# Ten input tiles scaled by VectorE in one instruction and transposed by DMA, in place of ScalarE, TensorE and a PSUM eviction

## What is computed

```python
def _rmsnorm(x, g):
    y = xf * lax.rsqrt(jnp.mean(xf * xf, axis=-1, keepdims=True) + EPS)
    return (y * g).astype(x.dtype)

u = _rmsnorm(h, g_mix)                       # D_MODEL = 1024
proj = jnp.einsum('ntd,de->nte', u, w_in)    # 1024 x 9216
a_b, a_c, a_h, a_z, b_v, b_g, b_z, gate_a, gate_b = jnp.split(proj, SPLITS, axis=-1)
v = b_v * jax.nn.sigmoid(b_g)                # input of the 31-tap convolution
...
h = h + m @ w_o
h = h + sigmoid(rmsnorm(h, g_ple) @ w_pg) * (p @ w_pe)
```

## Time and profile before

| | |
|---|---|
| median of 3 runs | 884.12 us (883.93 to 884.82) |
| the profiled execution | 888.18 us |
| its slowest core (core 1), first to last instruction | 886.6 us |
| TensorE busy | 855.5 us, 96% |
| VectorE, ScalarE, GpSimd busy | 508.5, 301.1, 145.0 us |
| shortest span of a core (core 0) | 877.5 us |

### The profile page before, as it was taken

How to read it: one execution, slowest core, us unless ns; L and a number is a source line. 1 busy time by engine, 2 the same in 40 slices (tenths; PEclk the granted TensorE clock), 3 DMA queues, 4 the chain that set the end, 5 groups by cost and what they waited for, 6 DMA issues and landing times.

```text
span 886.6 us, 15264 instructions; the slowest of 8 cores (877.5 to 886.6 us)
## 1 busy us (share of the span) xinstructions
PE 855.5 (96%) x4970; PEld 443.1 (50%) x4970; DVE 508.5 (57%) x791; ACT 301.1 (34%) x565; POOL 145.0 (16%) x274
## 2 busy tenths in 40 slices
PE   7999988999999999999999999999999999999993
PEld 4886544555444545454554444444445444444441
DVE  2455334566997777777777733333333235777775
ACT  4773223355344332423323321111111112444442
POOL 3142101100101101010210101110001001344441
PEclk9999999999999999999999999999999999999997
DMA  9977999987302123030313155521222044867642
GB/s 196 260 145 100 163 154 193 148 134 110 81 0 48 24 37 60 13 61 1 60 17 57 18 161 95 96 39 33 48 48 42 13 96 101 207 172 181 175 126 95
DMA packets 93964, 84.42 MB, mean 95 GB/s; under 512 B 53280, under 2 KB 74784, under 8 KB 93344
## 3 DMA queue, kind: packets, MB, share of 16 engines
q1 hardware_dynamic: 66112, 52.29, 25.2%
q0 software_dynamic: 27776, 31.17, 23.8%
HBM read 86.80 MB, written 15.61 MB: 116 GB/s over the span
## 4 chain that ended last, share of the span: by engine, by line
PE 85%; DMA 5%; SPq 3%; issue 2%; ACT 2%; DVE 2%; POOL 1%; DVEq 0%; POOLq 0%; ACTq 0%
PE ps L409 67%; PE ps L849 7%; PE ps L870 6%; SPq L346 3%; PE ps L604 3%; PE ps L876 1%; DMA t_v<-vd 1%; DMA vd<-t_vrow 1%; DMA t_x<-x 1%; PE ps L672 1%; DMA t_ring<-w_ob 1%; ACT t_xb L484 0%; PE ps L498 0%; DMA t_cb<-t_c 0%; ACT t_xb L424 0%
## 5 line engine op out<-in xcount | busy, mean ns | idle before, releaser
L409 PE MATMUL ps<-t_uT,t_ring 128*128 128x512 bf16 (+2 forms) x3200 | 543.5, 330 | 0.9 <-DMA t_ring<-w_in 0.7
L409 PEld LDWEIGHTS ps<-t_uT,t_ring 128*128 128x128 bf16 x3200 | 279.6, 98 | 252.5 <-issue 3.0
L823 DVE TENSOR_TENSOR t_tmp<-ps,t_tmp 128x512 f32<-128x512 f32 (+1 forms) x80 | 48.7, 610 | 151.7 <-PE ps L409 151.1
L343 POOL DMA_DIRECT2D t_ring<-w_in x72 | 38.8, 540 | 392.4 <-PE ps L409 389.6
L820 ACT ACTIVATE t_tmp<-ps 128x512 f32<-128x512 f32 (+1 forms) x80 | 42.3, 532 | 177.6 <-PE ps L409 177.6
L781 ACT ACTIVATE t_tmp<-t_tmp,t_vid 128x512 f32<-128x512 f32 (+1 forms) x40 | 29.9, 749 | 125.0 <-DVE t_tmp L778 125.0
L535 DVE TENSOR_TENSOR t_vrow<-ps,t_tmp 128x512 bf16<-128x512 f32 (+2 forms) x52 | 25.2, 485 | 79.1 <-PE ps L409 34.1
L409 PE MATMUL ps<-t_cb,t_ring 128*128 128x512 bf16 (+1 forms) x320 | 65.4, 347 | 0.3 <-DMA t_ring<-w_ob 0.3
L409 PE MATMUL ps<-t_yaT,t_ring 128*128 128x512 bf16 (+1 forms) x320 | 65.4, 347 | 0.0
L849 PE MATMUL ps<-t_wo_t,t_cb 128*128 128x512 bf16 x272 | 61.5, 379 | 0.0
L870 PE MATMUL ps<-t_wpg_t,t_u2T 128*128 128x512 bf16 x256 | 57.9, 379 | 0.0
(11 more groups left out here) (99 smaller groups left out, 755.1 us busy)
## 6 DMA issues: line engine op xcount, KB each, us to landing
t_ring<-w_in POOLq DMA_DIRECT2D x72, 256.0 KB, 5.9
t_x<-x SPq DMA_DIRECT2D x17, 512.0 KB, 8.6
t_xs<-x SPq DMA_DIRECT2D x17, 512.0 KB, 5.7
t_cb<-t_c SPq DMA_DIRECT2D x64, 128.0 KB, 6.5
y<-t_yt SPq DMA_DIRECT2D x16, 512.0 KB, 3.7
vd<-t_vrow SPq DMA_DIRECT2D x28, 128.0 KB, 4.6
t_v<-vd SPq DMA_DIRECT2D x7, 512.0 KB, 10.1
t_ring<-w_oa POOLq DMA_DIRECT2D x8, 256.0 KB, 5.9
```

Source lines behind the costliest of these rows:

```text
L343: S.add("pool", lambda e: e.dma_start(out=out, in_=in_), reads=reads, writes=list(writes) + [swq()], dma=key)
L409: S.add("pe", lambda e, k=k: e.matmul(ps[:, b, 0:n], lhsT=ring[k_ring][:, k, :], rhs=rhs_fn(k), start=(k == 0), stop=(k == NCH - 1)), read ...
L823: S.add("dve", lambda e, p=p, t=t: e.tensor_tensor(out=tmp[t][:, 0:n], in0=ps[:, p, 0:n], in1=tmp[t][:, 0:n], op=ALU.mult), reads=[f"ps{p} ...
```

## The change

From preparation step i = 7 on (tiles 6 to 15, ten tiles) `s1_a2` has a new body and `s1_b` returns at once. VectorE multiplies the float32 tile by the column `rsd` and by the row `g_mix` in one instruction and writes bf16 into `xb1`; after the load six steps ahead, SyncE issues a DMA transpose of `xb1` into the tile's columns of `uT`. The row of `g_mix`, broadcast to 128 partitions on the host, is a new input of 512 KB; it is loaded once by SyncE right after `s1_a2(1)`, into memory that the accumulators `accs`/`accq` use later. The first seven steps stay as they were.

`s1_step` now calls `s1_a2(i)` and `s1_a1(i + 1)` for i from 9 on; steps 8's scaling and 9's squares have moved into `FIRST`. The eight steps are called one after the other at P0 j=0, P0 j=2, P1 j=0, 1, 2, P2 j=0, 2, and P3 j=0 (ten calls before, the last at P3 j=2).

```diff
+        gmix = at("gmix", [128, D], F32, o_acc)
...
+        FIRST_DT = 7
...
         def s1_a2(i):
...
+            if i >= FIRST_DT:
+                t = TILES[i]
+                si, o = t // 4, 128 * (t % 4)
+                S.add("dve", lambda e: e.scalar_tensor_tensor(
+                    out=xb1[bq][:], in0=xs1[xq][:], scalar=rs_ap, in1=gmix[:], op0=ALU.mult, op1=ALU.mult),
+                    reads=[f"x1{xq}", rs_res, "gmix"], writes=[f"xb1{bq}", f"xb1h{bq}"])
+                if xnext[0] < len(TILES):
+                    s1_load(xnext[0])
+                S.add("sp", lambda e: e.dma_start_transpose(out=uT[si][:, :, o:o + 128], in_=xb1[bq][:]),
+                      reads=[f"xb1{bq}", f"xb1h{bq}"], writes=[f"uT{t}", f"uTh{t}"], dma=f"uT{bq}")
+                return
...
+            if i == 1:
+                sdma(gmix[:], gmix_d, [], ["gmix"], "gmix")
 
         def s1_b(i):
+            if i >= FIRST_DT:
+                return
...
-        nxt = [7]
+        nxt = [9]
 
         def s1_step():
             i = nxt[0]
-            if i < len(TILES):
-                nxt[0] += 1
-                s1_b(i)
-                s1_a2(i + 1)
-                s1_a1(i + 2)
+            nxt[0] += 1
+            s1_a2(i)
+            s1_a1(i + 1)
...
-                 (s1_a2, 6), (2, 4), (3, 0), (s1_b, 6), (s1_a1, 7), (3, 1), (s1_a2, 7), (3, 2), (s1_a1, 8), (3, 3), (3, 4)]
+                 (s1_a2, 6), (2, 4), (3, 0), (s1_b, 6), (s1_a1, 7), (3, 1), (s1_a2, 7), (3, 2), (s1_a1, 8), (3, 3), (s1_a2, 8),
+                 (s1_a1, 9), (3, 4)]
...
-        PIECES += [(1, 0, 256, (1, 0, 1, 0)), (1, 256, 256, (1, 1, 1, 0)), (2, 0, 256, (1, 1, 0, 1)),
-                   (2, 256, 256, (1, 0, 1, 0)), (3, 0, 512, (0, 0, 0, 0))]
+        PIECES += [(1, 0, 256, (1, 0, 1, 0)), (1, 256, 256, (1, 1, 1, 0)), (2, 0, 256, (1, 0, 1, 0)),
+                   (2, 256, 256, (1, 0, 0, 0)), (3, 0, 512, (0, 0, 0, 0))]
```

More of the change, by code:

```diff
@@ L180, in build_program @@
     gple_d = din("gple", [128, D])
+    gmix_d = din("gmix", [128, D])
     gfin_d = din("gfin", [128, D])
@@ L1052, in build_program @@
                 sdma(hista[:], sa_d, [], ["hista"], "hista")
+        assert nxt[0] == len(TILES)
         S.alias([f"cq{q}_{g}" for q in range(4, 8) for g in range(NQ)] + [f"c{q}_4" for q in range(4, 8)], X1_RES)
+        S.alias([f"acc{c}{si}" for c in "sq" for si in range(5)], ["gmix"])
         jobs = [(j, si) for j in range(4, 8) for si in (4, 0, 1, 2, 3)]
@@ L1237 @@
     gple = np.ascontiguousarray(np.broadcast_to(f(g_ple[0])[None, :], (128, D)))
+    gmix = np.ascontiguousarray(np.broadcast_to(f(g_mix[0])[None, :], (128, D)))
     gfin = np.ascontiguousarray(np.broadcast_to(f(g_final)[None, :], (128, D)))
@@ L1248 @@
     shared = dict(w_in=cols(w_in[0]), w_oa=cols(w_out_a[0]), w_ob=cols(w_out_b[0]), w_o=rows(w_o[0]),
-                  w_pg=rows(w_pg[0]), w_pe=rows(w_pe[0]), tw=tw, mask=mask, vecs=vecs, gfin=gfin, gple=gple)
+                  w_pg=rows(w_pg[0]), w_pe=rows(w_pe[0]), tw=tw, mask=mask, vecs=vecs, gfin=gfin, gple=gple, gmix=gmix)
     def phases(a):
```

## The result

The changed kernel takes **891.36 us** (median of 5 runs, 890.08 to 908.53) against 884.82 for the kernel before beside it (also 5 runs). In the longest run two cores of one die had a mean granted clock of 0.96 where the others had 0.99, so the ratio is taken from the other four: 1.0068, 95% interval 1.0054 to 1.0082. That is 6.0 us slower where 4.9 less was forecast. What TensorE was to save it did save. The waits for transposes came larger than priced and in more places, and the row of `g_mix` cost more.

What follows compares the result with a forecast made beforehand. TensorE was taken to set the pace; -6.3 us for removed transposes, +0.2 for the row of `g_mix` and +1.2 for the wait before P4 gave -4.9, so 884.12 became 879.2 us, range 876.5 to 885.0.

Steps and rivals of the forecast that it cites:

- The rest ... 6.3 us is what ten tiles cost: TensorE, 42.50 us to the last removed transpose's end: 30.74 less 24.43 of projections saves 6.3 us, at least 4.5.
- VectorE 1.28 us, ScalarE relieved: Ten VectorE evictions of 1.214 us become instructions of 1.278, 0.6 us more but hidden; ScalarE loses 11.5 us, adding no gain.
- these instructions now stand in front of later products: On VectorE, a late new instruction holds back products and PSUM banks; TensorE runs four projections, 7 us, ahead before that costs.
- The row of `g_mix` ... 0.2 us: 512 KB load on the x queue delays the loads behind it 2.4 us; cost 0.2 us, bounds nothing and 2.4.
- A queue that has little else to do: SyncE's queue takes ten transposes of 1.22 us issue time, 12 us; a `vst` store goes out about 1.2 us later.
- The tiles before the last have at least one more projection of lead: P1's transposes go out before P0; for P2 and P3 five projections or more lie between issue and need.
- The wait before P4: TensorE waits for the last tile's transpose at the start of P4: 1.2 us, bounds 0.2 and 4.5.
- It fits, but barely: DMA time in the shortened stretch: 28.9 us plus 11.7 for ten transposes, 40.6 us in 32, a share of 1.27.
- rival 1: DMA engines overfull in the shortened stretch, TensorE waits at P2, P3 and P4; about 883.5 us, no change; chance 0.16.
- rival 2: Last tile's transpose caught behind other packets at P4's start, TensorE waits 11.2 us; 889.2 us, slower; chance 0.12.
- Two signs that the text names against itself: Forecast is wrong if TensorE waits for `uT` at P2 or P3 too, or transposes take 9 us or more.
- Everything after P4 moves forward as it is: After P4 start, later loads and stores are issued when TensorE, ScalarE and VectorE reach them, so all moves forward.

Runs made afterwards that it cites:

- nosws: Changed kernel with mask, `tw`, `vsd` stores, history and `vs` loads behind the last transpose, and transposes ahead of x loads on SyncE; 1.0113 to the kernel before.
- dt11: Changed kernel, only steps 11 to 16 by DMA, GpSimd's loads early, `g_mix` behind step 8, scratch for squares, steps packed into P0 to P2; 0.9968, 882.8 us.
- dt9: dt11 with eight tiles by DMA (steps 9 to 16) and `g_mix` behind step 6; 1.0034 to the kernel before.
- dt11n: dt11 with `mask`, `tw` and the history in their old place after P0; 1.0020 to the kernel before.
- nosw: Changed kernel with mask, `tw`, `vsd` stores and loads of history and `vs` behind the last transpose; 1.0133 to the kernel before.
- bearly: Kernel before, with only the early loads of `mask`, `tw` and history, behind the squares of step 5; 0.9993 to the kernel before.

## Why the prediction was wrong

- **"The rest ... 6.3 us is what ten tiles cost": right.** Eight of the ten tiles lay between P1 and P4. The kernel before takes 28.1 us from the one to the other and nosws 22.9: 5.2 us, 0.65 a tile for the 0.63 of the text. dt11, with six tiles, takes 23.9: 4.2 us, 0.70 a tile.
- **VectorE 1.28 us, ScalarE relieved: right.** 1.280 us measured, ScalarE 10.0 us less busy on core 1 (291.1 for 301.1; the text has 11.5). That VectorE's new work is hidden held in its sum but not in its order: "these instructions now stand in front of later products" looked at what stands behind them. What stands before them is a product that a store of `vst` can hold. It did so for 2.03 us before P4 on core 1, hidden there behind SyncE's queue, and it is on the chain of dt9.
- **"The row of `g_mix` ... 0.2 us": mis-sized.** It measured 1.9 us with an interval of 0.3 to 3.6, near the upper bound of 2.4 in the text. With the row alone P1 to P4 already come 1.2 to 1.4 us later, so the stretch did not take up the delay; the range had it, the sum did not.
- **"A queue that has little else to do": wrong.** The ten transposes held SyncE for 22 to 29 us in sum, by core, where the text had 12. The median was 2.3 to 2.4 us on cores 0 and 1, the longest 10.9, and stores, loads and the next transpose stood behind it. On core 1 this put the last transpose's issue 1.65 us behind its tile.
- **"The tiles before the last have at least one more projection of lead": the step that failed most.** P1 was 2.9 us later than before (1.1 of it already at P0), and TensorE waited 1.5 to 2.8 us in front of it on every core; in front of P2 it waited on seven of eight, 0.6 to 2.2 us and 9.23 on core 0. The lead itself was there: step 8's transpose was issued 3.7 to 4.9 us before P1 was due. But P1 began only 5.6 to 7.5 us after that issue. The lead had been set against a landing of 2.9 us, from the last stage of one core, where one transpose was in flight at a time; on the other cores some take up to 5.3 even there. The median landing in this stretch was 5.2 to 6.0 us.
- **The wait before P4, taken as 1.2 us in bounds of 0.2 to 4.5.** Seven cores waited 2.5 to 3.9 us, inside the bounds but near their upper end. For the median core the P3 to P4 distance grew from 8.7 to 12.0 us.
- **"It fits, but barely": the size was right, the conclusion wrong.** The share was worked out at 1.27 and measured at 1.21 on core 1 (1.11 on core 0). What failed is the reading of a share as room. From 36 to 74 us TensorE is busy 33.6 of 38 us on core 1 at 1.21, but only 26.0 on core 0 at 1.11; in dt11 it is busy 35.5 to 37.8 at 0.96 to 1.09, in dt11n 31.2 to 34.8 at 0.96 to 1.16. So the share does not tell the loss; what is in flight together does. In the same way the 1.26 of the earlier trace rows was neither a licence nor a price: from 110 to 160 us the cores besides 1 and 4 of the kernel before have 1.20 to 1.33 and lose 0 to 2.3 us.
- **The rivals.** Rivals 1 and 2 were each half of it: engines overfull (rival 1) and a transpose caught behind others (rival 2, landings to 16.8 us, with 8.8 given as the point where the gain ends). Rival 2 looked for this at the start of P4 alone, and neither had SyncE's issue time in it. Two signs that the text names against itself came: a wait at P2, and landings of 9 us or more (cores 0 and 7). The Trainium skill's figure of 1309 ns for a 128x128 block (VectorE: DVE Perf Modes, The three transpose paths) would have made, as an estimate, 10.5 us a tile. No run bears it out as a price of the transpose itself: in dt11 the medians are 3.3 to 4.5 us.
- **"Everything after P4 moves forward as it is": right within 3 us** where GpSimd's loads were not moved behind P4, and the traces say no more than that. The changed kernel's median core is 4.2 us late at P4 and 5.9 at the last stage; dt11 is 4.2 early at both. It is wrong where loads are moved behind P4 (nosw, nosws).

The runs settle where the loss comes from for dt11n and dt11: GpSimd's loads beside transposes. Without transposes the place of the same loads makes no difference (bearly, 0.9993). For all ten tiles nosw shows that 8.3 us at P4 go with GpSimd's traffic, and the others show the jam following `tw`, the history and the x loads. But no version with ten tiles kept the gain to the end, so how the 10.9 us between forecast and result (6.0 lost, 4.9 promised) split between these, the row of `g_mix` and VectorE's order is open. Why the changed kernel's two measurements differ (1.0068 and 1.0094, with intervals that overlap) is open too.

## What to carry to other kernels

A DMA transpose that replaces work on the bound engine pays only where little else is in flight beside it. List the transfers of the stretch with the new traffic, and take landing and issue time from a place in the trace that has the same company, not from one where a transfer flew alone. A summed share does not replace this: it was 1.11 where core 0 of the changed kernel lost 12 us and 1.07 where core 4 of dt11 lost none. Count lead from the moment the data are ready after the worst hold of the engine that now prepares them, and through every issue that stands in front on the queue. If the gain is real but eaten, use the change on the part of the tiles that has the room: with six of ten it was 0.2 to 0.3% faster than the kernel before, with eight 0.3% slower.

## What the runs showed that was not expected

- Plain transfers and transposes slow each other down by more than they add: beside 1.05 MB on GpSimd's queue, transposes went from 4.0 to 8.1 us and stores from 2.7 to 7.6, at less data moved per time (158 for 183 GB/s from 54 to 72 us, core 4). Over all cores, the median landing of the 128 KB stores in these 18 us is 1.8 to 2.5 us with neither (bearly), 3.0 to 4.6 with GpSimd's transfers alone (the kernel before), 2.0 to 4.3 with transposes alone (dt11) and 4.7 to 7.6 with both (dt11n). The load of `tw` lands in dt11n about as before, in 9.3 to 11.7 us for 10.3 to 11.2: there it is the transposes and stores that give way. In the changed kernel it can be slow too, 16.4 us on core 0.
- The issue of a DMA transpose is not of fixed length: 1.22 us at the median in the last stage, up to 10.9 us on SyncE with `tw`, a load of x and other transfers in flight.
- A 512 KB load near the start, which nothing reads, cost 0.2% of a kernel of 885 us (interval 0.03 to 0.41%).
